# Moving two broadcast stores from the first attention stage to the start of the first up projection

## What is computed

```python
def first_block(x, ...):
    ...
    y_att = window_attention(q, k, v, sink[l])          # 6 heads, window 128
    y = concatenate([y_ssm, y_fft, y_att]) @ w_out[l]
    x = x + gt_m * rms_norm(y, g_post_mix[l])
    h = rms_norm(x, g_pre_ffn[l]) * (1.0 + sc_f) + sh_f
    up = dwconv3(h @ w_up[l], conv_w[l], conv_b[l])     # 2 x 2816 columns
    gate, val = split(up, 2)
    y = (gelu(gate) * val) @ w_down[l]
    x = x + gt_f * rms_norm(y, g_post_ffn[l])

def banded_attention(q, k, v, rel_bias, max_dist, stride):   # second block
    ...
    bias = rel_bias[t5_bucket(rel * stride)]
    logits = where(valid, logits + bias, NEG_INF)
```

## Time and profile before

| | |
|---|---|
| median of 3 runs | 3932.35 us (3929.28 to 3938.76) |
| the profiled execution's own time | 3929.27 us |
| its span in the profile | 3927.5 us |
| busy in the span: PE, PE weight load, DVE, ACT, POOL | 3391.6, 2811.4, 1193.1, 790.4, 1553.2 us |
| mean granted TensorE clock | 0.932 of full speed |
| HBM | 287.21 MB read, 55.95 MB written |
| DMA queue q1 (issued by SP) | 217784 packets, 258.76 MB, 21.8% of 16 DMA engines |
| DMA queue q10 (issued by ACT) | 43066 packets, 84.01 MB, 6.8% of 16 DMA engines |

### The profile page before, as it was taken

How to read it: one execution, slowest core, us unless ns; L and a number is a source line. 1 busy time by engine, 2 the same in 40 slices (tenths; PEclk the granted TensorE clock), 3 DMA queues, 4 the chain that set the end, 5 groups by cost and what they waited for, 6 DMA issues and landing times.

```text
span 3927.5 us, 41626 instructions
## 1 busy us (share of the span) xinstructions
PE 3391.6 (86%) x15935; PEld 2811.4 (72%) x15935; DVE 1193.1 (30%) x1793; ACT 790.4 (20%) x1395; POOL 1553.2 (40%) x1271
## 2 busy tenths in 40 slices
PE   6773335589999999999999999987778999999977
PEld 4663324477888878888888888876667788888866
DVE  4754664425232322110001123135534100001323
ACT  3020003423111112110000122035533100001222
POOL 3137662044333346622323664210015223236743
PEclk8886666889999999999999999999999999999999
DMA  4551001552111124311112243444433111122432
GB/s 174 149 183 36 7 7 42 87 152 75 43 54 43 54 95 140 102 54 54 43 53 77 96 142 122 143 134 110 108 101 108 49 54 43 53 74 98 151 107 95
DMA packets 261327, 344.92 MB, mean 88 GB/s; under 512 B 24710, under 2 KB 203185, under 8 KB 261202
## 3 DMA queue, kind: packets, MB, share of 16 engines
q1 hardware_dynamic: 217784, 258.76, 21.8%
q10 hardware_dynamic: 43066, 84.01, 6.8%
q0 software_dynamic: 352, 0.44, 0.0%
HBM read 287.21 MB, written 55.95 MB: 87 GB/s over the span
## 4 chain that ended last, share of the span: by engine, by line
PE 75%; DVE 11%; ACT 5%; issue 3%; DMA 3%; POOL 2%; SPq 1%; ACTq 0%; DVEq 0%; POOLq 0%
PE PS L810 68%; PE PS L1848 3%; DMA tab_bi<-bias 1%; DVE ot L1591 1%; PE PS L746 1%; DVE pl_ab L1956 1%; DVE pt L679 1%; PE PS L1543 1%; DVE oo L1592 1%; ACT ph_ab L1893 1%; ACT act L701 1%; DVE t L1607 1%; PE PS L1833 1%; ACT pr_ab L1883 1%; ACT act L653 1%
## 5 line engine op out<-in xcount | busy, mean ns | idle before, releaser
L250 POOL TENSOR_TENSOR w_lo<-w_raw,w_hi 128x512 fp32r<-128x512 f32 x724 | 972.2, 1374 | 155.1 <-ACT w_hi L1302 130.4
L246 POOL CAST w_hi<-w_raw 128x2048 fp32r<-128x2048 f32 x173 | 335.6, 1940 | 1596.2 <-DMA w_raw<-ffn_w_gu 606.8
L810 PE MATMUL PS<-h_hi,w_hi 128*128 128x512 f32 x2482 | 803.2, 395 | 14.3 <-DVE h_lo L804 11.0
L810 PE MATMUL PS<-h_lo,w_hi 128*128 128x512 f32 x2482 | 795.7, 392 | 0.0
L810 PE MATMUL PS<-h_hi,w_lo 128*128 128x512 f32 x2482 | 795.7, 391 | 0.0
L810 PEld LDWEIGHTS PS<-h_hi,w_hi 128*128 128x128 f32 x2482 | 469.2, 189 | 114.6 <-DVE h_lo L804 15.6
L810 PEld LDWEIGHTS PS<-h_hi,w_lo 128*128 128x128 f32 x2482 | 469.2, 189 | 98.1
L810 PEld LDWEIGHTS PS<-h_lo,w_hi 128*128 128x128 f32 x2482 | 469.8, 189 | 95.2
L810 PE MATMUL PS<-w_hi,a_hi 128*128 128x512 f32 x1056 | 327.5, 392 | 11.0 <-DVE a_lo L876 7.2
L810 PE MATMUL PS<-w_lo,a_hi 128*128 128x512 f32 x1056 | 327.2, 391 | 0.0
L810 PE MATMUL PS<-w_hi,a_lo 128*128 128x512 f32 x1056 | 326.8, 391 | 0.0
(11 more groups left out here) (281 smaller groups left out, 3630.3 us busy)
## 6 DMA issues: line engine op xcount, KB each, us to landing
w_raw<-ffn_w_gu SPq DMA_DIRECT2D x88, 512.0 KB, 4.6
w_raw<-ffn_w_down SPq DMA_DIRECT2D x88, 512.0 KB, 4.3
w_raw<-w_up SPq DMA_DIRECT2D x44, 512.0 KB, 5.0
w_raw<-w_down SPq DMA_DIRECT2D x44, 512.0 KB, 4.2
xs<-px ACTq DMA_DIRECT2D x40, 512.0 KB, 2.7
w_raw<-w_out SPq DMA_DIRECT2D x32, 512.0 KB, 4.5
w_raw<-w_in SPq DMA_DIRECT2D x28, 512.0 KB, 5.3
px<-xs ACTq DMA_DIRECT2D x7, 2048.0 KB, 10.4
```

The lines of the kernel that those rows point to most:

```text
L246: e.tensor_copy(w_hi[b][:, 0:n], w_raw[b][:, 0:n]).then_inc(S("w_hi"), 1)
L250: op = e.tensor_tensor(w_lo[b][:, s], w_raw[b][:, s], w_hi[b][:, s].bitcast(F32), ALU.subtract)
L810: mm = e.matmul(o, a[ai], b[bi], start=start and first, stop=stop and end)
```

## The change

The two stores are issued, by ScalarE as before, after the output projection's part and before ScalarE's part of the first up projection. `tab_act` ends with the copy of the last piece; its store part becomes a function `tab_store_act`, called once, ahead of `up_act(e, 0)`. `out_act` no longer waits for `tb_st`. Instead `up_act(e, 0)` waits for it between chunk 11 and chunk 12: its 22 chunks are written as 12 (two turns of a hardware loop of 6) and 10 (written out), instead of 18 in three turns and 4 written out.

```diff
         def out_act(e, p):
             e.wait_ge(S("at_yl"), 6 if p == 0 else 22)
-            if p == 0:
-                e.wait_ge(S("tb_st"), 32)
             post_load_act(e, p)
...
-            repeat(e, FT, 6, chunk)
+            if f:
+                repeat(e, FT, 6, chunk)
+                return
+            repeat(e, 12, 6, chunk)
+            e.wait_ge(S("tb_st"), 32)
+            repeat(e, FT - 12, 6, lambda i, j, turn: chunk(i + 12, j, turn))
...
             e.activation(tst[k][:, c:c1], PS[0:16, 2 + q % 2, 0:c1 - c], ACT.Copy, scale=8.0).then_inc(S("tb_ev"), 1)
-            if q + 1 < len(PIECES):
-                return
+
+        def tab_store_act(e):
+
             e.wait_ge(S("tb_ev"), len(PIECES))
             for k, w in enumerate((W_A, W_B)):
                 r = slice(8 * k, 8 * k + 8)
...
                     if last > p:
+                        if f == 0:
+                            tab_store_act(e)
                         up_act(e, f)
                         down_act(e, p)
```

## The result

The changed kernel takes 3966.93 us in the median of 4 runs (3962.86 to 3972.20), the kernel before, run beside it, 3935.34 us: a ratio of 1.0083, 95% interval 1.0064 to 1.0102. The forecast was 3967 us. The profiled execution took 3972.20 us.

A forecast was written before the change was run, and what follows sets the result against it. TensorE bounds the kernel, so only its waits could change: 76 us lost in the up projection less 41 gained in the attention, +35 on the 3932.35 us median, gives 3967 us; range 3945 to 4000.

The forecast's parts named there:

- The attention, 41.1 us: First attention stage: with both stores gone, ScalarE's issue hold and two groups' load delays vanish, gaining 41.1 us.
- The three terms: Attention gain: ScalarE's idle time at its two issues, 11.1 us; excess of two groups with late loads, 14.3 and 15.7.
- late head: Attention: each of two heads whose queries and bias load while the stores run; their groups exceed 7.83 us by 14.3 and 15.7.
- the group's time: Attention on ScalarE: a group of four units every 7.83 us throughout, once the stores are gone.
- The length of the stores, 123.8 us: Moved stores in the up projection: 30.7 us for the first and 93.1 us for the second, on 8 DMA engines.
- One for one: Shared DMA engines, up projection: each 512-byte weight row waits for one store row, 0.24 us (first store) or 0.73 us (second).
- rival (a): Up projection: chunk 3's and 4's weights arrive in time, only ScalarE's 2.5 us lost, 3894 us; chance 0.18 with partial forms.
- Chunk 3 and chunk 4: Up projection: their weights land at 1040 and 1081 us, late for TensorE, which stands idle some 55 and 19 us.
- the time in which a new load gets nothing: DMA engines busy with a store: a new load stands some 10 us behind what they have already taken up.
- Rival (b): Up projection: weights held until the stores end, loss 98 us, net +57, 3989 us; chance 0.28.
- The clock after the stall, 2 us: Up projection: TensorE restarts after its halt at a granted clock of 0.61 for 4 us, costing 2 us more.
- Rival (c): Attention: loads stay late, so only ScalarE's 11 us are gained; net +65 us, 3997 us; chance 0.04.

## Why the prediction was right

**The attention, 41.1 us: measured 34.6.** The three terms went as said: no hold of ScalarE and no late head, at either place. The mis-sized term is the group's time, which I took as 7.83 us throughout. After the change every other group takes 9.2 to 9.3 us, because TensorE drops to its low clock during its product with the values. Four such groups of 1.4 us are 5.6 us. That it is the clock and not a wait is shown by the run with an eighth of the stores in the attention: there the group's product takes 2.4 us and not 3.9, with nothing awaited inside it in either, and ten groups take 79.2 us (696.34 to 775.52) where they take 85.3 in the kernel after (696.21 to 781.49). Why the clock falls in the one and not in the other was not tested. What is left of the gap is no term of the sum: the execution after reached the stage 1.9 us later (a group ends at 685.92 against 684.01, ahead of the stores), so the stage itself gave 36.5. A further 1.8 us are lost in the output projection.

**The length of the stores, 123.8 us: right.** 143 rows in 13 us are 11.0 per us, the rate of the earlier trace rows, with weight rows between them, and the whole ran 123.6 us (920.1 to 1043.7). The stores did not get slower.

**One for one: right**, and the step that everything hangs on. It is shown by the counts (143 against 143, 8 against 8 in 0.72 us, 324 against 324 with rows of 1536 bytes), by chunk 3's landing with those rows (972 us, for 973 worked out) and by the three times 3967, 3929 and 3897 us. The argument against the Trainium skill's rule (page DMA: Bandwidth & Descriptors, section Queues, rings and completion order) was weaker than I took it. The rule is that an engine drains a packet, typically 9 to 17 descriptors, before it changes queues. I let the load have 9 rows for one row of the store; but the store would have its 9 rows too, its turn would be nine times as long, and the stall would be about the same. So the counts that I had, 104 against 102, did not speak against the rule, and it gave no reason for rival (a). The stretches of 0.72 us decide it: what the rule calls a packet is, for these loads and stores on the two hardware queues, one row.

**Chunk 3 and chunk 4.** In the time of the kernel after, 32.8 us earlier, I had chunk 3's landing at 1007 us and chunk 4's at 1048; measured 1016.9 and 1046.3. So TensorE stood 63 and 5 us and not 55 and 19. The mis-sized term is the time in which a new load gets nothing: I had taken 10 us, and between 937 and 941 us 2 weight rows went beside 134 of the store, so the busy engines took up the weights some 14 us after the issue at 927.3. By the end of the first store they had done 330 rows, 41 an engine and not 52; the missing 11 at 0.73 us are 8 of the 10 us. Rival (b) had a grain of truth in this, and in another thing: the sync engine was held 22 to 46 us by single issues, which I had costed at nothing. It hardly mattered to the sum: chunk 4 had only the 27 us from 1016.9 to the stores' end for turns with the store, and what was left of it, some 90 rows an engine, took 3 us behind that.

**The clock after the stall, 2 us: it came twice.** Chunk 3 took 25.3 us from its weights to its end (1023.8 to 1049.1) and chunk 4 24.0, for 21.75: 3.5 and 2.2 us, 5.7 for the 2 in the sum. The stretch behind the first restart, columns as in the earlier trace rows:

```profile
1023.00:1029.00 6.00, 5.02 (x12) 3.96 (x13) 0.00 (x0) 0.00 (x0) 0.85 (x1) 0.50 0.53 61
```

**The sum.** Loss 76 us, measured 73.9: two stalls of 67.5 us where I had 74, and the clock 5.7 for 2. Gain 41.1, measured 32.8 at the start of the stage. Net 35, measured 41 by that point in the profiled execution and 32 between the medians; the median's agreement to a tenth of a us is luck, the steps agree to some 8 us. Rival (a) needed landings in time; it is what the cut and paced stores then brought about, at 3895 to 3897 us, for the 3894 worked out. Rival (c) fell with the late heads.

## What to carry to other kernels

Before a long store is moved into a stage that streams weights, count rows and not bytes: on the two hardware queues here, a load of many short rows waited for one row of the store at each of its own, on every engine that the store used. Either cut the long transfer's rows to the length of the load's and issue them a few at a time (issued at once, the same short rows held ScalarE 120 us and cost 1.9%), or break it into pieces that end within the load's spare time; both turned a loss of 0.8% into a gain of 0.9%. Or write less: an eighth of the repeats gave 3895 and 3891 us, no better than the others beyond the noise, and then it didn't matter where the stores stood.

## What was not expected of the hardware

An issuing engine is held by its own DMAs: four stores issued in a row held ScalarE 72.7 us at the last three, twelve held it 120 us, GpSimd stood 66 us ahead of its eighth in a row, and the sync engine was held up to 46 us by a load beside another queue's store. A new load got nothing for some 14 us on the engines that a store kept busy. The same rows of 1536 bytes went as packets of 1.5 KB on ScalarE's hardware queue (654 for 0.99 MB) and of 4.6 KB on GpSimd's software queue (223 for 1.03 MB). And with the stalls out of the attention, TensorE's granted clock was lower in every other group, which gave back some 6 of 41 us (the run with 512-byte rows, its stores moved too, shows the same groups); with an eighth of the stores in the attention it was not.
